# Heads of five stages of a retention/attention/expert step made inside the stages ahead of them

## The reference

```python
h = rmsnorm(x, norm1_w) * (1 + scale1) + shift1
proj = h @ w_in                      # 1024 x 2304: 8 query heads, 2 key/value heads, retention q, k, v, gate
q, k = rmsnorm(q), rmsnorm(k)        # per head of 64; the 2048 latent tokens get a 2-D rotation
att = softmax(q @ K.T / 8) @ V       # latent: 2048 own keys + 128 cached; context: its own 128
ret = bidirectional retention: a state of 4 heads x 64 x 128 per direction, chunks of 128 tokens,
      with tables exp(-exp(logit) * distance) per head as mask and as decay of keys, queries and state
x = x + gate1 * (concat(att, silu(g) * rmsnorm(ret)) @ w_out)
h = rmsnorm(x, norm2_w) * (1 + scale2) + shift2
aff = softmax(h @ w_router)          # 16 experts; each takes its 256 best latent and 16 best context tokens
y = (silu(h[idx] @ w_gate) * (h[idx] @ w_up)) @ w_down   # per expert, width 1024
x = x.at[idx].add(gate2 * gates * y);  out = rmsnorm(x, norm_f_w)
```

## Time and profile before

| what | value |
|---|---|
| median of 3 runs | 3318.91 us (3317.86 to 3319.41) |
| the profiled execution, its own time | 3313.68 us |
| its span | 3312.0 us |
| mean granted TensorE clock | 0.96 of full |
| PE busy | 3081.9 us, 93% |
| DVE, ACT, POOL busy | 1849.8, 1715.6, 420.1 us |
| DMA | 394.61 MB, mean 119 GB/s |

### The profile page before, as it was taken

One profiled execution on the slowest core, in us unless ns is written; L12 is line 12 of the kernel. 1 busy time (PEld: TensorE's weight loads), 2 busy tenths in 40 slices (PEclk: granted clock), 3 DMA queues, 4 the chain that ended last, 5 costly groups with the idle time before them and its releaser, 6 DMA issues. The chain is left out here.

```text
span 3312.0 us, 58734 instructions
## 1 busy us (share of the span) xinstructions
PE 3081.9 (93%) x21488; PEld 2804.2 (85%) x21488; DVE 1849.8 (56%) x3175; ACT 1715.6 (52%) x3375; POOL 420.1 (13%) x396
## 2 busy tenths in 40 slices
PE   8999997799999999999799748999999999999995
PEld 4788886688888888888688638999999999999995
DVE  3222226688888888888433474545454555545455
ACT  3222224577777777777443245545545445454544
POOL 0333334400000000000000010111111111111103
PEclk9999998899999999999899758999999999999998
DMA  6221115500000000000264115656666566666656
GB/s 235 75 75 64 64 61 177 181 14 26 22 20 27 19 22 22 25 22 20 71 203 152 64 53 196 189 184 186 185 186 187 183 189 186 183 191 187 189 166 262
DMA packets 318188, 394.61 MB, mean 119 GB/s; under 512 B 30132, under 2 KB 274312, under 8 KB 317080
## 3 DMA queue, kind: packets, MB, share of 16 engines
q1 hardware_dynamic: 307160, 356.11, 32.5%
q0 software_dynamic: 10560, 36.77, 4.9%
q10 hardware_dynamic: 384, 0.62, 0.1%
HBM read 319.54 MB, written 74.06 MB: 119 GB/s over the span
## 5 line engine op out<-in xcount | busy, mean ns | idle before, releaser
L2557 DVE TENSOR_TENSOR e_w_lo<-e_raw,e_w_hi 128x2048 fp32r<-128x2048 f32 x192 | 440.2, 2292 | 487.5 <-ACT e_w_hi L2487 487.5
L93 PE MATMUL e_ps<-e_x_hi,e_w_hi 128*128 128x272 f32 x2048 | 602.3, 294 | 5.5 <-issue 5.5
L95 PE MATMUL e_ps<-e_x_hi,e_w_lo 128*128 128x272 f32 x2048 | 593.9, 290 | 0.0
L94 PE MATMUL e_ps<-e_x_lo,e_w_hi 128*128 128x272 f32 x2048 | 590.3, 288 | 0.0
L1559 DVE TENSOR_TENSOR a_pT_lo<-a_ps_t,a_pT_hi 128x512 fp32r<-128x512 f32 (+1 forms) x648 | 368.4, 601 | 138.1 <-ACT a_pT_hi L1457 137.7
L1457 ACT ACTIVATE a_pT_hi<-a_ps_t 128x512 fp32r<-128x512 f32 (+1 forms) x648 | 319.6, 532 | 171.0 <-PE a_ps_t L1321 166.0
L93 PEld LDWEIGHTS e_ps<-e_x_hi,e_w_hi 128*128 128x128 f32 x2048 | 386.4, 189 | 7.1 <-issue 5.5
L94 PEld LDWEIGHTS e_ps<-e_x_lo,e_w_hi 128*128 128x128 f32 x2048 | 387.1, 189 | 0.0
L95 PEld LDWEIGHTS e_ps<-e_x_hi,e_w_lo 128*128 128x128 f32 x2048 | 386.2, 189 | 0.0
L2487 ACT ACTIVATE e_w_hi<-e_raw 128x2048 fp32r<-128x2048 f32 x192 | 366.1, 1907 | 14.5 <-DMA e_raw<-in_w_gate 10.1
L1532 DVE TENSOR_REDUCE a_mx<-a_ps_s 128x1 f32<-128x896 f32 (+2 forms) x392 | 346.5, 892 | 22.6 <-PE a_ps_s L1311 22.6
(11 more groups left out here) (310 smaller groups left out, 5345.9 us busy)
## 6 DMA issues: line engine op xcount, KB each, us to landing
e_raw<-in_w_gate SPq DMA_DIRECT2D x64, 1024.0 KB, 5.0
e_raw<-in_w_up SPq DMA_DIRECT2D x64, 1024.0 KB, 5.0
e_raw<-in_w_down SPq DMA_DIRECT2D x64, 1024.0 KB, 5.0
s_ret<-p_pr SPq DMA_DIRECT2D x17, 768.0 KB, 3.6
p_raw<-in_w_in SPq DMA_DIRECT2D x8, 1152.0 KB, 18.9
o_cT<-s_ct SPq DMA_DIRECT2D x17, 512.0 KB, 5.1
s_x<-o_x SPq DMA_DIRECT2D x17, 512.0 KB, 5.0
s_xn<-o_xn SPq DMA_DIRECT2D x17, 512.0 KB, 3.5
```

The lines of the kernel that those rows point to most:

```text
L93: nc.tensor.matmul(out, w_hi, x_hi, start=first, stop=False)
L94: nc.tensor.matmul(out, w_hi, x_lo, start=False, stop=False)
L95: return nc.tensor.matmul(out, w_lo, x_hi, start=False, stop=last)
L2557: nc.vector.tensor_tensor(w_lo[n % RING][:, :, :], raw[n % RING][:, :, :], w_hi[n % RING][:, :, :].bitcast(F32), ALU.subtract).then_inc(w_ ...
```

## The change

It moves work, and changes no arithmetic. In order of the program:

1. `clear` and its blocks are gone. `set_back` has SP clear the semaphores of the stage before somewhere in the present stage's list; those of the last stage are not cleared.
2. The retention tables are made in `project`: the iotas on POOL at the start, the loads on SP ahead of the tiles, the rest on DVE and ACT at the start of the context tile. The cached keys and values are copied early, too, and of the context tile's stores that of `s_ret` goes first. `project` no longer waits for its stores: `retention` waits on SP, for the latent tiles' stores first and for the context tile's where it needs them. The load of the given states comes behind the first tile's keys and values.
3. A class `FirstKeys` holds attention's keys, values and first queries at an address of their own. SP loads them in `retention`, between the third `load_qk` and the fourth, and clears 72 semaphores behind that. ACT makes the high parts at the ends of tiles 1 (queries), 2, 3 and 12 (keys); DVE makes the low parts of two chunks within tiles 15 and 16, the rest after tile 16.
4. `attention` loads the first two `o_cT` tiles and the router weights in its context tile. `retention`, `attention` leave the wait for their last stores to the next stage.
5. A class `FirstWeights` holds the experts' weight rings and `e_xg`. SP loads the first four chunks and ACT makes three high parts in `selection`; its last act is expert 0's gather on POOL, started as soon as `token` is written.
6. At the experts' start ACT turns out the even row chunks and DVE the odd ones, and the rows are split in two halves; DVE makes two low weight parts ahead of that and the third behind it.

The diff, cut to its core:

```diff
-    def clear(self):
-        with self.nc.Block() as block:
-            @block.sync
-            def _(sp):
-                for sem in self.own:
-                    self.nc.sync.sem_clear(sem)
+def set_back(nc, spent):
+    for sem in spent:
+        nc.sync.sem_clear(sem)
@@ project
+            sp.dma_start(s["kv"][NT, :, 0:KV_W], a["cache_attn_k"]...)   # and the values, lg, cdl
             over_tiles(sp, body)
-            sp.dma_start(s["kv"][NT, :, 0:KV_W], a["cache_attn_k"]...)
-            sp.wait_ge(qk_out, 32 * NTA)
-            sp.wait_ge(rest_out, 32 * NTA)
-            sp.wait_ge(ctx_out, 64)
             def body(h, j, i):
+                if is_ctx(i):
+                    decay_exponentials()      # ACT;  on DVE: decay_tables()
@@ retention, SP
+            sp.wait_ge(g["projected"]["rest"], 32 * NT)
+            over_quads(sp, load_quads)
...
             load_qk(0, 2)
+            sp.wait_ge(g["projected"]["qk"], 32 * NT)
+            sp.wait_ge(g["projected"]["ctx"], 112)
+            g["first"].load(sp)
+            set_back(nc, spent)
@@ retention, ACT
+                if known(h, off, 1):
+                    g["first"].queries_hi(act)
+                for n, t in enumerate((2, 3, NT - 4)):
+                    if known(h, off, t):
+                        g["first"].keys_hi(act, n)
@@ retention, DVE
+                for n, t in enumerate((NT - 1, NT)):
+                    if known(h, off, t):
+                        g["first"].keys_lo(dve, n)
             over_tiles(dve, body)
+            g["first"].queries_lo(dve)
+            g["first"].keys_lo(dve, 2)
@@ FirstKeys
+    def load(self, sp):
+        sp.dma_start(self.q_row[:, :, :].rearrange("p h f -> p (h f)"), self.s["q"][0]).then_inc(self.q_in, 16)
+        for n in range(self.n):
+            sp.dma_start(self.k_all[:, self.tiles(n), :], ...).then_inc(self.kv_in[n], 16)
+        sp.dma_start(self.v_all[:, :, :], ...).then_inc(self.v_in, 16)
@@ attention, SP
-            (the same five loads)
             for c in range(DC):
                 sp.dma_start(w_out[:, c, :], a["w_out"][0, c * P:(c + 1) * P, :]).then_inc(w_out_in, 16)
+            for sem, stored in g["retained"]:
+                sp.wait_ge(sem, stored)
+            sp.sem_inc(stored_ok, 1)
+            set_back(nc, spent)
...
+                if isinstance(i, int) and i == NT:
+                    sp.wait_ge(att_out, 16 * (NT - 1))
+                    for n in range(2):
+                        sp.dma_start(g["heads"][n]..., s["ct"][n]).then_inc(g["heads_in"][n], 16)
+                    sp.dma_start(g["router"][:, :, :], ...).then_inc(g["router_in"], 16)
@@ selection
+            for n in range(g["weights"].RING):          # SP
+                g["weights"].load(sp, n)
+            set_back(nc, spent)
+            pool.wait_ge(token_ok, 1)                    # POOL, last
+            g["weights"].gather(pool, s["xn"].rearrange("t p d -> (t p) d"), g["token"])
+            for n in range(g["weights"].RING - 1):      # ACT, ahead of the ranks
+                g["weights"].high(act, n)
@@ experts, ACT
-            for n in range(AHEAD):
-                split(0, n)
-            for c in range(DC):
+            for c in range(0, DC, 2):
                 rows(0, c)
-            rows_hi(0)
+            act.wait_ge(xT_ok, 2 * DC)
+            nc.scalar.activation(x_hi[:, 0:DC // 2, :], xT[:, 0:DC // 2, :], ACT.Copy).then_inc(x_hi_half, 1)
+            nc.scalar.activation(x_hi[:, DC // 2:, :], xT[:, DC // 2:, :], ACT.Copy).then_inc(x_hi_ok, 1)
```

More of the change, by code:

```diff
@@ L523, in project @@
         blocks.close()
-        k.clear()
+        return k.own
 def over_pairs(eng, body, head, pairs, tail):
@@ L1223, in body @@
             def body(i):
-                if not (isinstance(i, int) and i == NT):
+                if isinstance(i, int) and i == NT:
+                    sp.wait_ge(att_out, 16 * (NT - 1))
+                    for n in range(2):
+                        sp.dma_start(g["heads"][n][:, :, :].rearrange("p c t -> p (c t)"), s["ct"][n]).then_inc(g["heads_in"][n], 16)
+                    sp.dma_start(g["router"][:, :, :], a["w_router"][0].rearrange("(c p) e -> p c e", p=P)).then_inc(g["router_in"], 16)
+                else:
                     for n in range(2):
@@ L1738, in _ @@
         def _(pe):
-            pe.wait_ge(wr_in, 16)
             def gates(who, out):
@@ L1924, in output_projection, with selection @@
         blocks.close()
-        k.clear()
-def selection(nc, g, a, s):
+        return k.own
+def selection(nc, g, a, s, marks, spent):
     with ExitStack() as ctx:
-        k = Core(nc, ctx)
+        k = Core(nc, ctx, marks)
         aff8, aff = g["aff"], g["aff"][:, :, 0, :]
@@ L2238, in selection, with __init__, chunk, load @@
         blocks.close()
-        k.clear()
-def experts(nc, g, a, s):
+        return k.own
+class FirstWeights:
+    BC = 256
+    RING = 4
+    BELOW = 100352
+    def __init__(self, nc, k, a, xg_in):
+        self.nc, self.a = nc, a
+        with ExitStack() as above:
+            k1 = Core(nc, above)
+            k1.sb("e_below", [P, self.BELOW // 4])
+            self.raw = [k1.sb(f"e_raw{i}", [P, DC, self.BC]) for i in range(self.RING)]
+            self.w_hi = [k1.sb(f"e_w_hi{i}", [P, DC, self.BC], F32R) for i in range(self.RING)]
+            self.w_lo = [k1.sb(f"e_w_lo{i}", [P, DC, self.BC], F32R) for i in range(self.RING)]
+            self.xg = k1.sb("e_xg", [P, 3, D])
+        self.w_in, self.w_hi_ok, self.w_lo_ok = k.sems("e_w_in", self.RING), k.sem("e_w_hi_ok"), k.sem("e_w_lo_ok")
+        self.xg_in = xg_in
+    def chunk(self, n, e):
+        w = (self.a["w_gate"], self.a["w_up"])[n % 2] if n < 8 else self.a["w_down"]
+        b = n // 2 if n < 8 else n - 8
+        w = w[0, e] if isinstance(e, int) else w[0, bass.ds(e, 1)].rearrange("a k n -> (a k) n")
+        return w.rearrange("(c p) n -> p c n", p=P)[:, :, b * self.BC:(b + 1) * self.BC]
+    def load(self, sp, n):
+        sp.dma_start(self.raw[n][:, :, :], self.chunk(n, 0)).then_inc(self.w_in[n], 16)
+    def high(self, act, n):
+        act.wait_ge(self.w_in[n], 16)
+        self.nc.scalar.activation(self.w_hi[n][:, :, :], self.raw[n][:, :, :], ACT.Copy).then_inc(self.w_hi_ok, 1)
+    def gather(self, pool, xn_rows, token):
+        for n, m in enumerate([P, P, CAP_CTX]):
+            pool.indirect_dma_start(self.xg[0:m, n, :], None, xn_rows,
+                                    bass.IndirectOffsetOnAxis(ap=token[0:m, 0, n:n + 1], axis=0)).then_inc(self.xg_in, 16)
+def experts(nc, g, a, s, marks, spent):
     with ExitStack() as ctx:
-        k = Core(nc, ctx)
-        BC = 256
-        RING = 4
+        k = Core(nc, ctx, marks)
+        early = g["weights"]
+        BC, RING = early.BC, early.RING
         PER = 3 * FF // BC
```

377 lines of the change are left out of this document (209 added, 168 removed).

## The result

| | before | changed |
|---|---|---|
| median, four runs each | 3318.39 us (3313.76 to 3319.41) | 3281.76 us (3279.58 to 3283.02) |
| ratio of the runs, 95% interval | | 0.9897 (0.9885 to 0.9910) |
| the profiled execution, own time (span) | 3313.68 (3312.0) | 3282.97 (3281.2) |

The change is faster by 36.6 us in the medians, 1.0%, and by 30.7 us between the two profiled executions, of which the old one was the fastest of its kernel and the new one near the slowest. Forecast were 3277.3 us (3267 to 3292) and 41.6 of gain. The working is judged by stretches of the traces, each from the instruction of the row above to the one named, in us. Tiles count from 0, so that tile 16 is the last, the context's.

What follows compares the result with a forecast made beforehand. PE bounds the kernel, so the gain is its shorter waits between stages: 9.4 - 4.0 - 0.5 + 11.5 + 7.8 + 1.9 + 12.6 + 2.9 = 41.6 us, from 3318.91 to 3277.3 us (3267 to 3292).

Steps and rivals of the forecast that it cites:

- The seams: Stage starts and program end: gains of 9.4 (retention), 11.5 (attention), 7.8 (output projection), 1.9 (selection), 12.6 (experts), 2.9 us (end).
- uncharged 10.7: Start of retention: PE starts 10.7 us earlier, before charging the given states' load, which left 9.4.
- Inside retention: -4.0 and -0.5 us: Retention's loop: 4.0 us lost once as tile 3's queries wait behind clears and 2.6 MB, 0.5 for ACT's splits.
- DVE's splits in tiles 15 and 16 take 1.76 us, in a gap that was 2.29 us: nothing: End of retention's loop: DVE's key splits fit into its idle gap and cost nothing.
- Seam 2, 11.5 us: Retention into attention: first scores at 639.4 against 650.92, after DVE's splits and PE's 80 transposes; ends 13.6 and 5.0.
- the rival that they don't bring the clock up: Attention's start: transposes don't raise PE's clock, so it gives 5.0 instead of 11.5 us; 3284; chance 5%.
- Seam 5, 12.6 us: Selection into experts: early gather and halved splits put the first product at 1988.9 against 2001.41; ends 8.5 and 16.
- The shorter price beside it: Experts' start: the Trainium skill's about 2.0 us for a small GpSimd transfer, said to make the sum 2.5 us more.
- The loads choke retention: Retention's loop: 2.6 MB and 72 clears cost 12 us and more, later loads being late in turn; 3287; chance 12%.
- Only the clears go: All stage starts: only 250 clears leave the path, 16 us, heads being bound by something else; 3303; chance 6%.
- The half clock in expert 0: Experts' start: PE stays at half clock over expert 0, 38 us slower, 3357; chance 3%.
- What was to show it: Signs in the changed profile: first scores some 16 us earlier, `o_c_hi` some 24, first expert product some 38.7.

Runs made afterwards that it cites:

- e1: Changed kernel, but retention's SP clears the 72 semaphores in tile 15, not ahead of tile 3's load; 3282.82 us.
- e8: Changed kernel, but attention's queries, keys and values are loaded and split at attention's start again, clears staying in retention; 3278.99 us.
- e6: Changed kernel, but attention's loads spread in pieces over retention's tiles, ACT's high parts in tiles 3, 12, 13, 14, clears in tile 15; 3274.02 us.
- e2: Changed kernel, but all three low parts of the keys made behind retention's loop, none within tiles 15 and 16; 3282.71 us.
- e10: Changed kernel, but expert 0's gather is POOL's first act in the experts' block, not its last in the selection; 3287.38 us, two runs.
- e5: Changed kernel, but its 210 clears stand in blocks of their own between the stages and behind the last; 3295.27 us.
- e7: Changed kernel, but DVE makes two low weight parts at the selection's end, behind a semaphore step after POOL's gather; 3280.39 us.

## Why the prediction was right, and where its steps were not

- **The seams.** Output projection, selection and program end came within 0.1 us, the start of retention within 0.1 of the uncharged 10.7. The reading (the first useful instruction of a stage hangs on SP's clears, and where it needs one on a load behind them) holds. The price of a clear was a little high, 0.06 to 0.065 us against 0.054 in SP's records. Those of the kernel before part the 2.24 us that the prediction couldn't: 1.66 for the 31 clears and 0.29 for each of the two edges, as taken.
- **"Inside retention: -4.0 and -0.5 us"** is the step that failed most: +8.6 in the second loop where 4.5 was charged, and +2.7 ahead of it where 1.3 was charged (in the eleven other traces +0.8 to +3.3, cause open). The stall's place and cause by name were right (tile 3's queries, a DMA), its size 5.8 and not 4.0. Of its two stated causes the clears were none (e1; in e8 they stand alone and the loop is as before), the bytes all (e6). ACT's splits, charged with 0.5, cost nothing: the loop takes 69.97 us with them (e6) and 69.92 without (e8).
- **"DVE's splits in tiles 15 and 16 take 1.76 us, in a gap that was 2.29 us: nothing"** is wrong by 2.9 us. The gap was DVE's, but it lay there because DVE waited for POOL, and the split stopped POOL (e2): the row that the prediction read names POOL as what ended it.
- **Seam 2, 11.5 us:** 10.1. The 80 transposes and the last copy took 12.5 us, not 11.1. When the granted clock rises differs between executions of the same kernel: the windows of PE in the changed kernel and, below, in its repetition, each from PE's first transpose on (clock: the third number from the end):

```profile
630.63:635.63 5.00, 5.00 (x23) 0.50 0.82 313
635.63:636.63 1.00, 1.00 (x8) 0.61 1.04 422
```

```profile
628.45:630.45 2.00, 2.00 (x9) 0.50 0.64 212
630.45:631.45 1.00, 1.00 (x6) 0.57 0.93 344
631.45:632.45 1.00, 1.00 (x11) 1.00 0.99 406
```

  At half clock for over 5 us in the one, for under 3 in the other, where the seam is 11.5 us shorter than before, as forecast. Both rise while PE does transposes only, so the rival that they don't bring the clock up is out.
- **Seam 5, 12.6 us:** 10.2. "DVE's two low weight parts are done before the rows come" failed: the block's edge waited for the gather (e10), and DVE began at 1961.24. I had counted POOL's transfer as in flight across the edge. So an engine other than the gather held part of this start (PE's 2.52 us for DVE), which the prediction had named as a sign of being wrong. The gather itself was priced about right: its third part landed 4.5 us behind its start, against 4.9, and the edge came 0.5 us behind that. The shorter price beside it would have made the sum 2.9 us more, not the 2.5 written there, and no trace has it.
- **The other rivals.** "The loads choke retention" had the cause right (the bytes), but not the repetition: it is a single stall, and its price of 12 us was twice the 5.8 that the loop lost to the loads. "Only the clears go": putting 210 of them back costs 13.2 us in the stretches (e5), and the heads are the rest of the gain. The half clock in expert 0 did not stay. The chances of the faster cases add up to 97%, where the last line of the chances has 94.
- **What was to show it.** The first scores came 7.8 us earlier and not 16, `o_c_hi` 14.7 and not 24, the first expert product 27.2 and not 38.7. Of the 11.5 us that are missing at that last point about half are retention's.
- **The level.** The projection ends 1.6 us later. In twelve traces with this projection its end lies between 500.9 and 504.5 us, so that an execution alone moves it by more; but the one trace before, with 500.7, lies ahead of all twelve. Whether a part of the 1.6 us is the change's stays open.
- **Luck.** The time fell within 4.5 us of the forecast since the medians moved 6 us further than the profiled pair did. By the traces alone the gain was overrated by 10.9 us: 5.6 in retention, 2.4 at the experts' start, 1.4 at attention's, and 1.6 in the projection. That more than half of this was made up by the level of the executions is luck.

## What to carry over

A gap of an engine may be filled only if what ends the gap doesn't need what the filler takes: DVE's splits with two operands in SBUF held up POOL, also where POOL gathers. A head that is loaded early is best loaded in pieces between the loads of the loop that hosts it; in one go 2.6 MB cost 5.8 us, in seven pieces nothing. What one stage leaves in flight on POOL was paid at the block's edge, so work that should run beside it belongs ahead of that edge.

## What the runs showed of the hardware that I had not expected

- POOL's 128x4 power took 2.44 us and not 1.01 beside a DVE subtraction of two SBUF operands; its indirect gathers took 2.02 and 1.81 us and not 0.95 and 0.86. A gather that had begun before the split kept its 1.22 us (e7).
- A semaphore clear took SP 0.054 us, the extra edge of a block 0.23 to 0.28 us at three of five seams (e5).
- SP needed 4.09 us to start a load of 256 KB behind 2.6 MB just started, against 0.33 to 0.61 for the others of that trace. 72 clears in that time cost nothing.
- A block ended only when POOL's gather had landed: its edge 8.06 us behind the token numbers with a gather in flight, 1.2 without. A bare semaphore step on POOL was seen by DVE within 0.5 us of the first gather's start, long before POOL was through.
